# A hybrid decoder trunk with 32 experts: the down weights' load moved between the two halves of the next expert's first-layer load

## What is computed

```
g_idx = jnp.argmax(g_logits, axis=-1)
top_v, top_i = lax.top_k(e_logits, TOP_K_IN_GROUP)
...
act = jax.nn.silu(xb @ w_gate[e]) * (xb @ w_up[e])
return act @ w_down[e]
```

## Time and profile before

| what | value |
|---|---|
| median of 3 runs | 1160.08 us (1155.35 to 1160.58) |
| the profiled execution | 1157.44 us |
| its span | 1155.7 us |
| TensorE busy | 1035.5 us (90% of the span) |
| weight loads in section 6 | 64 up, 64 gate, 32 down |
| queue of SP, bytes | 234.78 MB |

### The profile page before, as it was taken

The page is one execution under the profiler, slowest core; times in us unless marked ns, Lnnn a source line. Parts: engine busy times, 40 slices in busy tenths (PEclk is TensorE's granted clock), DMA queues, the critical chain, the costliest instruction groups (busy, mean ns, idle before and its releaser), DMA issues.

```text
span 1155.7 us, 20667 instructions
## 1 busy us (share of the span) xinstructions
PE 1035.5 (90%) x6564; PEld 496.6 (43%) x6564; DVE 735.0 (64%) x1704; ACT 564.0 (49%) x1213; POOL 421.5 (36%) x317
## 2 busy tenths in 40 slices
PE   5999999999999999998799977764999987989893
PEld 5898444446445656565533322211233322323230
DVE  3470009973555665626689966644899877878692
ACT  3221110114565555621278855533788766767571
POOL 0101089970010001010226553422656554545452
PEclk9999999999999999998899988897999998989896
DMA  8126111101251110129696899999979999999910
GB/s 270 24 39 119 37 37 37 37 15 58 79 212 62 56 55 19 55 96 376 227 408 229 292 407 409 414 408 415 405 272 404 412 412 413 403 414 414 405 59 33
DMA packets 89238, 258.22 MB, mean 223 GB/s; under 512 B 36467, under 2 KB 53626, under 8 KB 64542
## 3 DMA queue, kind: packets, MB, share of 16 engines
q1 hardware_dynamic: 67636, 234.78, 52.7%
q0 software_dynamic: 15776, 21.04, 6.4%
q10 hardware_dynamic: 5706, 0.92, 0.5%
HBM read 248.79 MB, written 30.41 MB: 242 GB/s over the span
## 4 chain that ended last, share of the span: by engine, by line
PE 66%; DMA 22%; issue 3%; DVE 3%; ACT 2%; SPq 2%; POOL 1%; ACTq 0%; POOLq 0%; DVEq 0%
PE psum L1157 14%; PE psum L1467 14%; DMA W<-in_w_gate 9%; PE psum L1355 9%; DMA W<-in_w_down 7%; PE psum L1490 6%; PE psum L1154 5%; DMA x_rows<-RD,tabf 4%; PE psum L1300 3%; PE psum L1320 3%; PE psum L1152 3%; PE psum L1311 2%; PE psum L1384 1%; PE psum L1448 1%; SPq L575 1%
## 5 line engine op out<-in xcount | busy, mean ns | idle before, releaser
L1050 ACT ACTIVATE RD<-W 128x512 f32 (+1 forms) x328 | 201.1, 628 | 145.0 <-POOLq L761 86.2
L1983 DVE COPY W<-W 128x1024 f32 x328 | 219.5, 712 | 82.2 <-POOLq L761 64.2
L1467 PE MATMUL psum<-W,band 128*32 x320 | 154.9, 630 | 42.1 <-DVE W L1983 40.9
L1467 PE MATMUL psum<-W,RD 128*32 (+1 forms) x336 | 160.6, 623 | 21.7 <-DVE W L1983 21.7
L1157 PE MATMUL psum<-W 128*128 128x512 f32 x384 | 166.9, 593 | 0.4 <-ACT W L876 0.4
L1490 PE MATMUL psum<-W,RD 128*32 (+1 forms) x328 | 154.4, 614 | 11.8 <-DVE W L1987 8.6
L1468 PE MATMUL psum<-RD 128*32 128x512 f32 x336 | 160.6, 623 | 0.0
L1469 PE MATMUL psum<-W,RD 128*32 128x512 f32 x336 | 160.6, 623 | 0.0
L1470 PE MATMUL psum<-W,RD 128*32 128x512 f32 x336 | 160.6, 623 | 0.0
L1468 PE MATMUL psum<-RD,band 128*32 128x512 f32 x320 | 154.9, 630 | 0.0
L1469 PE MATMUL psum<-W,band 128*32 128x512 f32 x320 | 154.9, 630 | 0.0
(11 more groups left out here) (343 smaller groups left out, 2131.9 us busy)
## 6 DMA issues: line engine op xcount, KB each, us to landing
W<-in_w_up SPq DMA_DIRECT2D x64, 1024.0 KB, 15.9
W<-in_w_gate SPq DMA_DIRECT2D x64, 1024.0 KB, 19.5
W<-in_w_down SPq DMA_DIRECT2D x32, 2048.0 KB, 23.8
W<-in_x SPq DMA_DIRECT2D x16, 512.0 KB, 4.7
W<-in_w_in SPq DMA_DIRECT2D x5, 1024.0 KB, 11.8
W<-in_w_in SPq DMA_DIRECT2D x16, 256.0 KB, 4.4
x_rows<-W SPq DMA_DIRECT2D x8, 512.0 KB, 2.9
h_rows<-RD SPq DMA_DIRECT2D x8, 512.0 KB, 3.9
```

The costliest lines, as they stand in the source:

```text
L1050: act.activation(farA[j].rearrange("p (g n) -> p g n", g=2), src, ACT.Copy).then_inc(ex_cA, 1)
L1467: pe.matmul(out[0:SUB].rearrange("p (g n) -> p g n", g=2), xA, near, start=k == 0, stop=k == KD - 1)
L1983: dve.tensor_copy(bothB[j].rearrange("p (h g n) -> p h g n", h=2, g=2), src.rearrange("p g (h n) -> p h g n", h=2)).then_inc(ex_cB, 1)
```

## The change

In SP's loop over the places, the load of the down weights of place p-1 with its wait now stands between the two halves of the first-layer load of place p. Before, it stood behind both. Nothing else is changed.

```
                     gone[p] = last_of(p - SLOTS)
                     sp.wait_ge(ex_xT, sp.snap(gone[p] + 1))
                     load_upgate(p, 0)
-                    sp.wait_ge(ex_u, gone[p])
-                    load_upgate(p, 1)
                 if p > SLOTS:
                     sp.wait_ge(ex_y, gone[p - 1])
                     load_down(p - 1)
+                if p < EXPERTS:
+                    sp.wait_ge(ex_u, gone[p])
+                    load_upgate(p, 1)
```

## The result

| | median | lowest |
|---|---|---|
| before (20 runs) | 1157.43 us | 1154.39 |
| after (20 runs) | 1161.03 us | 1157.62 |

The ratio of after to before is 1.0040, with a 95% interval of 1.0029 to 1.0050: the changed kernel is 0.4% slower, 4.6 us by this ratio and 3.6 us by the two medians (1.0031). One run of each kernel, of 3346.2 us and 1544.43 us, is left out of the ratio as slow and hardly moves the medians. I had forecast 7.0 us, and 1167.1 us. Of the 6.1 us between that and the 1161.03 measured, 2.65 come from the base (the median of 3 runs, 1160.08, stood that much above that of 20), the other 3.4 from the change, whose price I set too high. The direction and the kind of loss were right; two terms of the sum were not.

What follows compares the result with a forecast made beforehand. A full weight-load stream, ending with the landing of place 30's first-layer weights, was taken to bound the kernel. Pause 3.05 + later landing 4.95 - clock 1.0 = 7.0 us on 1160.1 gave 1167.1 us, range 1161 to 1174.

Steps and rivals of the forecast that it cites:

- The order: In the full load stream, down weights land one transfer earlier and first-layer weights about 5.0 us later.
- The wait: Second first-layer half also waits for the former down layer; queue stock covers it (6.6 us at place 31), cost nothing.
- The gains at places 24 and 27: Waits of 4.23 and 5.76 us for down weights go, but later waits for first-layer weights swallow the gain.
- The pause: Load stream's pause around place 15 ends 3.05 us later: 5.0 later start of step 16, less 1.95 for down weights.
- a sign I had named for being wrong: The prediction is wrong if the load stream's pause, ending at 851.09, ends as before instead of at about 854.
- The end: Place 30's first-layer weights land 8.0 us later, 3.05 of it from the pause; the tail behind moves unchanged.
- 1.0 us given back by the clock: Before pair 37 a shorter wait leaves TensorE's clock less slowed: 1.0 us back, bounds 0 and 2.8.
- Rival A: Pause ends as now, perhaps by faster clock in steps 16 and 17; only the end moves, 4.0 us slower; chance 0.22.
- B: Not slower: the two outstanding transfers land together, the pause ends 1.95 us earlier, 1158 us; chance 0.05.
- D: Gains win: three waits for down weights, 12.9 us on VectorE, go unswallowed; some 6 us faster; chance 0.04.

Runs made afterwards that it cites:

- the four profiles with the old order: Kernel before, profiled twice (again: 1.0004), with only the added wait (0.9998), and with idle transposes ahead of steps 16 and 37 (1.0008).
- the four profiles with the new order there: Changed kernel profiled twice (1.0040, again 1.0034), with idle transposes ahead of steps 16 and 37 (1.0024), and new order only up to place 17 (1.0008).
- all three: Kernel before with the new order only at places 16, 24 and 27: 0.9977.
- the second profile: Kernel before run and profiled once more, unaltered: 1.0004.
- the second profile after: Changed kernel run and profiled once more, unaltered, against the kernel before: 1.0034.
- the three new profiles: Changed kernel profiled twice (1.0040, again 1.0034) and once with idle transposes ahead of steps 16 and 37 (1.0024).
- the four places: Kernel before with the new order only at places 16, 24, 27 and 31: 0.9948; with idle transposes ahead of steps 16 and 37: 0.9945.

## Why the prediction was right in kind and wrong in size

*The order: right.* Down weights for pairs at 830, 979 and 1031 are not waited for, first-layer weights are, later by about a transfer. With the new order from place 29 on alone, pair 37 starts at 1086.7 against a mean of 1081.6 in the four profiles with the old order: 5.1 us, where I had 4.95. At the other end step 16 starts 4.5 to 6.8 us later in the four profiles with the new order there, where I had 5.0.

*The wait: right in its price.* Measured by itself it was free (0.9998). In the new order the cover of 6.6 us at place 31 was too thin, the DMA share fell to 0.69 for 5 us, but nothing that TensorE waits for lay behind the hole.

*The gains at places 24 and 27: right.* Swallowed; place 16 alone gives what all three give.

*The pause: wrong, and the larger error.* The step reads: "so the wait for D(15) costs 1.95 us of it, and this goes". It was read from one execution. The four profiles with the old order (the first rows of the table) start step 18 at 837.0 in the mean, not 835.1, and with place 16 turned round alone at 832.8. So this wait costs some 4.2 us, idle time (2.55 us in the second profile) and clock together, not far from the 4.5 to 6.8 us by which step 16 starts later. The whole new order starts step 18 at 838.4 in the mean of three profiles, 836.4 in the one turned round only up to place 17. The pause itself, counted from step 3, ends at 853.4 in the second profile after and at 853.6 in the second before, so that a sign I had named for being wrong, a pause that ends as before, has nearly come. The term is 1.3 us (0.9 with that one) instead of 3.05, and 0.9 us by the timed runs.

*The end: a term missing.* I had the tail behind pair 37 move "as it stands", with 1.0 us given back by the clock. In the mean of the same profiles the new order is 5.6 us later at the start of step 37, 3.1 us later at step 39 and 3.8 us at the end. What is given back on the way has two parts. Step 37 gives back 0.5 us: it ran at full clock in two of the three new profiles, one of them with transposes (11.5 us, behind waits of 2.1 and 2.7 us), but in two of the four old ones as well. Step 38 gives back 2.0 us: in three of the four old profiles it was 12.4 to 14.0 us long for D(30), a wait that the new order takes away. The earlier trace rows hold no row of it, and I had read its 1.03 us as covered; this is the term that the sum lacks. Behind step 39 0.7 us are lost again, and no run shows to what.

The sum as measured is then 1.3 (the pause) + 4.3 (first-layer weights behind the pause) - 1.8 (step 37 to the end) = 3.8 us, against 3.9 and 4.6 us in the two timed comparisons. Rival A had the right total, 4.0 us, and nearly the right place, partly by luck: the pause was spared by the whole wait for D(15) that went, its idle time more than its clock, and step 16, on whose clock A also counted, stayed at 0.87 and 0.89. (The lower end of the range, 1161, was also mis-worked: A's 2 us on 1160.1 are 1162.) B was wrong in its mechanism: the transfers do land one behind the other. D was wrong for the change, but it had a grain: two of the waits for down weights (D(15) and D(30)) are worth up to 6 us where nobody waits for what is put back in their place, as the four places show.

That D(15) was waited for 1.4 us less in the first profile of before than in the second is its landing: 24.70 us from issue in the one, 26.21 in the other. Why one and the same load takes 1.5 us more stays open, and so does how much the holes in the queue add to the lateness of U(15).

## What to carry to other kernels

In a full load stream, an order is worth judging place by place: here a transfer put forward helped only where its wait led to a moment that isn't set by the stream (the end of a pause, and the tail), and it harmed where the one put back was waited for last. Turned round at 4 of 28 places the same edit made this kernel 0.5% faster, turned round at all of them 0.4% slower; which places these are depends on the sizes of the experts, here on this routing. And a term of 2 us read from one profiled execution is as uncertain as itself: a second profile of the kernel before would have changed two terms of the sum.

## What I had not expected of the hardware

The same step behind a wait took 11.5, 13.2 or up to 14.5 us, at a granted clock of 1.00, 0.87 and 0.79 to 0.80. In the 14 profiles I read steps 16, 28, 32, 36 and 37, leaving out those with transposes in or ahead of them. The length of the wait told which only roughly. Behind waits under 2 us a step always took 11.5. Behind 2.0 to 3.5 us it took now 11.5 and now 13.2 or 13.3, three times 14.3 or 14.4 (13.3 behind 2.0 us before step 36 in one profile, 11.5 behind 3.5 us before step 32 in another). Behind 3.6 us and more it always took 12.9 to 14.5. A wait of TensorE thus had a second price of 0 to 3.0 us here, which in the middle range can't be read off its length.
